# Differential attention loop: where VectorE's join of the preceding unit stands in a step

## What is computed

```python
def diff_attend(q1, q2, k1, k2, v, lam):
    scale = DIFF_QK_DIM ** -0.5
    s1 = jnp.einsum('bqhd,bkhd->bhqk', q1, k1).astype(jnp.float32) * scale
    s2 = jnp.einsum('bqhd,bkhd->bhqk', q2, k2).astype(jnp.float32) * scale
    p = jax.nn.softmax(s1, axis=-1) - lam * jax.nn.softmax(s2, axis=-1)
    return jnp.einsum('bhqk,bkhd->bqhd', p.astype(v.dtype), v)
```

## Time and profile before

| what | value |
|---|---|
| median of three runs | 3003.81 us (3001.68 to 3007.8) |
| profiled execution, span | 3003.8 us; the three runs' median is the same, so that nothing lies around the span |
| busy in the span | PE 94%, PEld 70%, DVE 47%, ACT 38%, POOL 8% |
| chain that ended last | PE 82%, DVE 7%, DMA 4%, ACT 4%, issue 2%, POOL 2% |
| loop in layer 0, first to last maximum | 1637.6 to 1724.2 us |
| loop in layer 1, first to last maximum | 2544.1 to 2602.7 us |

### The profile page before, as it was taken

The page is one execution under the profiler, slowest core; times in us unless marked ns, Lnnn a source line. Parts: engine busy times, 40 slices in busy tenths (PEclk is TensorE's granted clock), DMA queues, the critical chain, the costliest instruction groups (busy, mean ns, idle before and its releaser), DMA issues.

```text
span 3003.8 us, 40104 instructions
## 1 busy us (share of the span) xinstructions
PE 2816.4 (94%) x16212; PEld 2094.2 (70%) x16212; DVE 1422.1 (47%) x2150; ACT 1129.1 (38%) x1920; POOL 238.4 (8%) x229
## 2 busy tenths in 40 slices
PE   7999979989999979999999789999999999799998
PEld 5657854536658745447877578888888787578886
DVE  6665532237666333244555763333334654753444
ACT  4664431124665321135233652222222542643332
POOL 0011020000011110001011010000001111000001
PEclk9999989999999989999999899999999999999999
DMA  4011249981002259993435122223320234222220
GB/s 157 29 43 59 86 173 415 415 366 64 29 29 100 100 237 418 414 395 127 144 115 153 40 76 113 112 114 128 124 84 16 88 122 130 81 84 99 98 99 28
DMA packets 67909, 428.28 MB, mean 143 GB/s; under 512 B 7968, under 2 KB 8352, under 8 KB 20368
## 3 DMA queue, kind: packets, MB, share of 16 engines
q1 hardware_dynamic: 62144, 407.96, 35.6%
q0 software_dynamic: 4432, 15.67, 1.6%
q10 hardware_dynamic: 1152, 2.10, 0.2%
HBM read 416.78 MB, written 8.91 MB: 142 GB/s over the span
## 4 chain that ended last, share of the span: by engine, by line
PE 82%; DVE 7%; DMA 4%; ACT 4%; issue 2%; POOL 2%; SPq 0%; DVEq 0%; ACTq 0%; POOLq 0%
PE banks L854 78%; PE banks L855 4%; DMA weight<-in_w_up 3%; ACT arena L1685 3%; DVE arena L2390 3%; POOL arena L3200 2%; DVE arena L3046 1%; DVE arena L2679 0%; DVE weight_part L2494 0%; DMA block_tokens_high<-df_stage 0%; DVE arena L2677 0%; DMA weight<-in_ada_w 0%; ACT weight_part L1685 0%; DVE x L2390 0%; POOL block_tokens_low L3214 0%
## 5 line engine op out<-in xcount | busy, mean ns | idle before, releaser
L1685 ACT ACTIVATE arena<-banks 128x512 f32<-128x512 f32 (+2 forms) x513 | 281.2, 550 | 885.0 <-PE banks L854 779.4
L854 PE MATMUL banks<-weight,arena 128*64 128x512 f32 (+4 forms) x2136 | 429.1, 573 | 21.3 <-DMA weight<-in_w_up 9.2
L854 PE MATMUL banks<-hidden,weight_part 128*128 128x512 f32 (+1 forms) x2304 | 446.8, 355 | 0.0
L854 PEld LDWEIGHTS banks<-hidden,weight_part 128*128 128x128 f32 x2304 | 381.2, 189 | 70.4 <-issue 3.8
L854 PE MATMUL banks<-tokens_high,weight_part 128*128 128x512 f32 (+1 forms) x1536 | 409.0, 357 | 10.0 <-ACT tokens_high L1685 10.0
L2494 DVE TENSOR_TENSOR weight_part<-weight,weight_part 128x2048 fp32r<-128x2048 f32 x124 | 285.8, 2308 | 194.8 <-ACT weight_part L1685 194.7
L1685 ACT ACTIVATE weight_part<-weight 128x2048 fp32r<-128x2048 f32 x124 | 236.4, 1908 | 349.7 <-PE banks L854 336.4
L854 PEld LDWEIGHTS banks<-weight,arena 128*64 128x64 f32 (+2 forms) x2136 | 150.9, 135 | 255.4 <-issue 233.8
L854 PEld LDWEIGHTS banks<-tokens_high,weight_part 128*128 128x128 f32 x1536 | 273.9, 190 | 62.5 <-DVE arena L2390 16.0
L3200 POOL TENSOR_TENSOR arena<-arena 128x512 f32<-128x512 f32 (+1 forms) x89 | 116.0, 1303 | 1974.3 <-ACT arena L1685 1707.4
L854 PE MATMUL banks<-tokens_low,weight_part 128*128 128x512 f32 (+1 forms) x768 | 264.7, 354 | 0.0
(11 more groups left out here) (216 smaller groups left out, 3879.6 us busy)
## 6 DMA issues: line engine op xcount, KB each, us to landing
weight<-in_w_gate SPq DMA_DIRECT2D x64, 1024.0 KB, 13.6
weight<-in_w_up SPq DMA_DIRECT2D x64, 1024.0 KB, 8.1
weight<-in_w_down SPq DMA_DIRECT2D x64, 1024.0 KB, 11.2
weight<-in_w_ff SPq DMA_DIRECT2D x64, 1024.0 KB, 4.8
weight<-in_ada_w SPq DMA_DIRECT2D x48, 1024.0 KB, 6.3
weight<-in_w_in SPq DMA_DIRECT2D x28, 1024.0 KB, 5.2
weight<-in_w_o SPq DMA_DIRECT2D x8, 1024.0 KB, 4.8
weight<-in_w_mem_kv SPq DMA_DIRECT2D x8, 1024.0 KB, 4.9
```

The source lines that it names most:

```text
L854: mm = lambda o, a, b, first=True, last=True: eng.matmul(o, a, b, start=first, stop=last, skip_group_check=True)
L1685: act = lambda o, i, f=ACT.Copy, **k: eng.activation(o, i, f, **k)
```

## The change

VectorE's stream alone changes. In each step the join of unit i-1, with the reciprocal of row sums that may follow it, moves behind the maximum over S(i,1). No instruction is added or taken away, and the other engines' streams stay as they were.

```diff
--- before.py
+++ after.py
@@ -3095,11 +3095,6 @@
                         split_low(("w_out", l, 3))
                     if i < len(us):
                         df_top(us[i], 0)
-                    if 1 <= i <= len(us):
-                        u = us[i - 1]
-                        df_join(u)
-                        if df_ends(u):
-                            shares(df_okey(u), S, [])
                     for (j, side), n in df_post_at(l).items():
                         if n and i == n + j and side <= both:
                             df_post(j, side)
@@ -3107,6 +3102,11 @@
                             df_gain(j, side)
                     if i < len(us):
                         df_top(us[i], 1)
+                    if 1 <= i <= len(us):
+                        u = us[i - 1]
+                        df_join(u)
+                        if df_ends(u):
+                            shares(df_okey(u), S, [])
                     if DF_LAG + 1 < i and df_ends(us[i - DF_LAG - 2]):
                         u = us[i - DF_LAG - 2]
                         c = int(u[0] == "dc")
```

## The result

The changed kernel takes 3014.36 us (median of six runs, 3009.53 to 3017.98) beside 3004.99 us before on the same chips (3001.31 to 3009.32). The ratio is 1.0027, 95% interval 1.0017 to 1.0038: slower by some 8 to 9 us. The forecast was 3014.8 in a range of 3005 to 3024. The profiled execution of the changed kernel has a span of 3011.3 us, 7.5 us over that of before. Each execution that is on record with its span took 1.7 to 1.9 us longer than it (this one 3013.08 us), so a little time does lie around the span.

What follows compares the result with a forecast made beforehand. The loop was taken as bound by a ring over VectorE and ScalarE, replaced by one through TensorE. Opening 7.2, first join 1.5, full-clock steps 2.0, closing -2.6 and half-clock steps 2.9 gave 11.0 on 3003.8: 3014.8 us, range 3005 to 3024.

Steps and rivals of the forecast that it cites:

- What bounds the loop: Loop before: VectorE and ScalarE set 3.40 us a step; once values are computed, TensorE joins in, 7.08 us per two steps.
- The ring of before: Loop before: join, maximum over the second half, its exponential, next join; one turn 3.40 us, without TensorE.
- The new ring and its two prices: Changed loop: join, transposes, second-half scores, their maximum, next join; 3.64 us at the full clock, 4.60 at the half.
- Opening and first join: Each layer's start: three half-clock steps add 3.6 us; first join waits for a fourth maximum, 0.73; both layers 7.2 and 1.5.
- Full-clock steps: Wide steps with TensorE at the full clock: 0.20 us more a pair, ten of sixteen pairs taken, 2.0 us.
- Closing: End of each layer's loop: the last two joins follow each other closer, -1.3 us a layer, -2.6 in both.
- What I costed at nothing: Narrow units and steps with norm parts: no cost; changes there by microseconds would show the prediction wrong.
- More steps at the half clock: Wide steps without values outside the opening: three more fall to the half clock, 0.96 us each, 2.9 us.
- The faster one: Rival for the wide steps: VectorE alone sets 3.28 us a step, about 8 us saved, 2996 us; chance 0.07.
- The rival with the full clock: Rival: opening keeps the full clock, costing 1.4 us instead of 7.2, no half-clock steps added, 3006 us; chance 0.20.
- the one with twelve more steps at the half clock: Rival for wide steps without values outside the opening: twelve instead of three, 11.5 us instead of 2.9, 3023 us; chance 0.13.

Runs made afterwards that it cites:

- the added matmul: One matmul of 512 columns put ahead of the second-half scores in wide steps from the third on, against the kernel before: 3008.48 us, ratio 1.0012.

## Why the prediction was right

**What bounds the loop.** Right. The ring of before ran over VectorE and ScalarE: its steps took 3.39 to 3.40 us at either clock, and the added matmul left the third opening step at 3.40. At the half clock there was less room beside it than this says: the second step grew by 0.17 us.

**The new ring and its two prices.** Right: 3.64 and 4.60 us were forecast from rows of before, 3.65 and 4.61 measured, and a matmul added to it lengthened it by its own length.

**Opening and first join.** Right: 4.61, 4.61 and 4.62 us in layer 0 in place of 3.40, 3.39 and 3.40, which is 3.65 a layer in both layers (forecast 3.6). One premise was read too widely: in layer 1 TensorE was at the half clock in only two of the three steps before (the earlier trace rows ends ahead of the third). In the changed kernel it was there in all three, as the sum assumed. The first maximum and the first join stand 1641.11 - 1637.49 = 3.62 us apart in layer 0, 0.73 more than before, as forecast. In layer 1 it is 1.09 more; the fourth maximum there also waited 0.43 us for its scores.

**Full-clock steps.** Right in size, 0.2 us a pair, but not in number. Ten pairs were counted, 2.0 us; layer 1 has five such steps in a row, which cost 0.7 us together, and layer 0 hardly any.

**Closing.** -1.41 us in layer 1 (forecast -1.3); in layer 0, whose loop ends with narrow units, only -0.41, since the last two joins there stood 1.97 us apart before and not 3.40.

**What I costed at nothing.** Here the prediction was wrong. It named changes by microseconds in the narrow units and the norm steps as a sign against it, and they came. The steps around the narrow units gave back about 1.2 us at the first place and 0.8 at the second, both in layer 0. The norm steps cost 2.04 us (layer 0) and 3.22 (layer 1) where they stand. In layer 0 the steps behind gave this back to within 0.1 us, in layer 1 2.2 of it. Most of that came from two steps with values, of the kind for which no difference was counted: before they took 5.77 us at a clock of 0.50, in the changed kernel 4.26 at 0.77 and 3.66 at 0.96.

**More steps at the half clock.** Three were assumed, 2.9 us. In the profile one wide step without values was added near 4.6 us, the fifth of layer 0 (4.61 in place of 3.39). The thirteenth of layer 1 stands at 4.61 as well, but took 4.71 before. The steps right behind the opening, in which the clock comes back, cost 0.29 and 0.53 more. Together that is some 2.0 us.

**The sum.** 11.0 us forecast, 9.4 between the medians. In the profiles the loops grew by 3.4 us (layer 0) and 4.9 (layer 1) from first maximum to last join, and about 0.9 came back outside, for which no run has a cause. Since executions of one kernel lie some 8 us apart, one profile of each cannot settle the smaller terms. The opening's 7.3 us is the one large term, and it was right. The rest came out near its forecast because errors of opposite sign met; that 3014.36 lies within 0.5 us of 3014.8 is luck.

**The rivals.** The faster one failed at the place that was named: T and S(i,1) together do not fit under a maximum, and scores do not pass a waiting T. With the order of TensorE and ScalarE turned as well, the norm parts last and two buffers more, something near its result came: 2997.55 us where 2996 was given for it. The sizes were others (steps of 3.11 us without values and 3.56 with them in layer 1, not 3.28 in all), so the number is partly luck. The rival with the full clock failed on the opening's 0.50, and the one with twelve more steps at the half clock on the single one that was added.

## What to carry to other kernels

In a loop of several engines, look for the rings: write down which instruction of one step releases which of the next, on every engine and through every buffer, and add each ring up. Moving an instruction behind another opens one ring and closes another, and the longest one decides; here the join lost its place ahead of a maximum and gained the transposes and scores of TensorE. In this loop, taking the two maxima in a row gained only once TensorE and ScalarE took both halves in a row too, with buffers to match.

## What was not expected

Two buffers that were worth nothing in one order (ratio 1.0027 without them, 1.0030 with them) were worth some 17 us in another (1.0070 and 1.0011). A ring's price can also hide a clock: 3.40 us a step at either clock before, 3.65 or 4.61 after, with the same work on TensorE.
